# A two-layer transformer block on one core: the norm's root moved to the FFN's eviction, the shift as extra columns, and constant products on TensorE

## The reference

```
def rms_norm(x, w):
    return x * rsqrt(mean(x * x, axis=-1) + 1e-6) * w
def modulate(h, shift, scale):
    return h * (1.0 + scale) + shift
def swiglu(h, w_in, w_out):
    gate, up = split(h @ w_in, 2, axis=-1)
    return (silu(gate) * up) @ w_out
h = h + 0.5 * lm[2] * swiglu(modulate(rms_norm(h, norm_w), lm[0], lm[1]), ffn_w_in, ffn_w_out)
```

## Time and profile before

| | us |
|---|---|
| median of 3 runs | 2743.12 (2735.91, 2743.12, 2744.52) |
| profiled execution, its own time | 2739.12 |
| its span | 2737.2 |
| TensorE matmul busy | 2664.7 (97%) |
| VectorE busy | 1521.2 (56%) |
| ScalarE busy | 692.3 (25%) |
| mean granted TensorE clock | 0.992 of full |

### The profile page before, as it was taken

How to read it: one execution, slowest core, us unless ns; L and a number is a source line. 1 busy time by engine, 2 the same in 40 slices (tenths; PEclk the granted TensorE clock), 3 DMA queues, 4 the chain that set the end, 5 groups by cost and what they waited for, 6 DMA issues and landing times.

```text
span 2737.2 us, 42267 instructions
## 1 busy us (share of the span) xinstructions
PE 2664.7 (97%) x15515; PEld 2290.5 (84%) x15515; DVE 1521.2 (56%) x2621; ACT 692.3 (25%) x1075; POOL 93.7 (3%) x211
## 2 busy tenths in 40 slices
PE   7999999999999999999999999999999989999998
PEld 4888888888877888888888888888887877888886
DVE  5776477534376477626763677247536465543333
ACT  4111111122256221111111311111113345422222
POOL 0000000000034000000000000000000022000000
PEclk8999999999999999999999999999999999999999
DMA  7877477412200177536762577257422200233332
GB/s 228 198 184 185 113 184 184 125 50 79 54 17 2 54 165 185 146 86 159 184 161 58 123 184 175 71 140 184 126 70 84 69 26 17 81 96 100 91 110 81
DMA packets 485795, 316.98 MB, mean 116 GB/s; under 512 B 30588, under 2 KB 483664, under 8 KB 485712
## 3 DMA queue, kind: packets, MB, share of 16 engines
q1 hardware_dynamic: 485712, 315.88, 45.2%
HBM read 313.73 MB, written 2.10 MB: 115 GB/s over the span
## 4 chain that ended last, share of the span: by engine, by line
PE 91%; DVE 4%; ACT 2%; issue 1%; POOL 1%; DMA 0%; SPq 0%; DVEq 0%; ACTq 0%; POOLq 0%
PE pg L709 79%; PE pg L776 4%; PE p L1047 1%; PE pn L1030 1%; PE pg L986 1%; PE p L724 1%; DVE xlo L1640 1%; DVE tnorm L1632 1%; PE pg L867 1%; ACT whi L1155 0%; DVE wlo L1493 0%; PE pg L991 0%; DVE probT L1847 0%; DVE mx L1854 0%; ACT xhi L1244 0%
## 5 line engine op out<-in xcount | busy, mean ns | idle before, releaser
L709 PE MATMUL pg<-xhi,whi 128*128 128x512 f32 (+1 forms) x2856 | 794.5, 347 | 4.1 <-DVE wlo L1493 4.0
L709 PE MATMUL pg<-xhi,wlo 128*128 128x512 f32 (+1 forms) x2856 | 788.6, 344 | 0.0
L709 PE MATMUL pg<-xlo,whi 128*128 128x512 f32 (+1 forms) x2856 | 787.1, 344 | 0.0
L1155 ACT CAST whi<-raw 128x1024 fp32r<-128x1024 f32 (+1 forms) x288 | 321.8, 1118 | 1060.2 <-PE pg L709 1045.9
L1493 DVE TENSOR_TENSOR wlo<-raw,whi 128x1024 fp32r<-128x1024 f32 (+1 forms) x288 | 377.6, 1311 | 350.5 <-ACT whi L1155 347.8
L709 PEld LDWEIGHTS pg<-xhi,whi 128*128 128x128 f32 x2856 | 451.3, 188 | 72.6 <-DVE wlo L1493 5.9
L709 PEld LDWEIGHTS pg<-xlo,whi 128*128 128x128 f32 x2856 | 450.4, 188 | 69.3
L709 PEld LDWEIGHTS pg<-xhi,wlo 128*128 128x128 f32 x2856 | 450.4, 188 | 68.9
L1577 DVE SCALAR_TENSOR_TENSOR part<-ada,cond,part 128x256 f32<-128x256 f32 x960 | 465.3, 485 | 32.7
L1703 DVE SCALAR_TENSOR_TENSOR h<-pg,gcol,h 128x512 f32 (+1 forms) x118 | 71.4, 639 | 442.3 <-PE pg L709 437.5
L709 PE MATMUL pg<-ahi,whi 128*128 128x512 f32 x1100 | 306.1, 346 | 0.0
(11 more groups left out here) (212 smaller groups left out, 1983.4 us busy)
## 6 DMA issues: line engine op xcount, KB each, us to landing
ada<-in_w_ada SPq DMA_DIRECT2D x512, 256.0 KB, 4.2
raw<-in_ffn_w_in SPq DMA_DIRECT2D x176, 512.0 KB, 3.9
raw<-in_ffn_w_out SPq DMA_DIRECT2D x64, 704.0 KB, 4.5
raw<-in_w_in SPq DMA_DIRECT2D x24, 512.0 KB, 3.8
ada_first<-in_w_ada SPq DMA_DIRECT2D x8, 1024.0 KB, 11.9
raw<-in_w_in SPq DMA_DIRECT2D x16, 256.0 KB, 3.5
raw<-in_w_o SPq DMA_DIRECT2D x16, 256.0 KB, 2.8
raw<-in_w_o SPq DMA_DIRECT2D x32, 128.0 KB, 2.9
```

Source lines behind the costliest of these rows:

```text
L709: last = nc.tensor.matmul(pg[s][:, p0:p1], w[:, s, k], v[:, k, p0:p1], start=(k == 0 and n == 0), stop=(k == kt - 1 and n == 2))
L1155: nc.scalar.copy(whi[:, s, 0:nk], raw[:, s, 0:nk]).then_inc(s_whi[s], 1)
```

## The change

For the norms 0, 2 and 3 (`POST`), the operand of the FFN's first product is `h * acol` without the root and the shift; `xhi` and `xlo` get two more columns with the shift vectors (latent and context), so that columns 768 and 769 of `pg` receive `shift @ w_in`. Every matmul of the second token part in these phases has 258 columns in place of 256. The root is multiplied in when the product is read, and the shift product is added as a bias per partition. `square_sums` of part 1 moves behind the whole first token part, and the roots come at the end of the norm on ScalarE. For norm 3, six of the eight tiles of `xhi` and `xlo` are made during the last pair of the phase before (`EARLY_K`); for norm 2, whose `xhi` is still being read by the product before, from the end of its first token part on. The rows of `xhi` and `xlo` grow from 768 to 776 elements.

In the opening ScalarE squares the untransposed input, with a sum per token; VectorE spreads it over a diagonal, so that `square_sums` gives the same; VectorE copies five of six transposed tiles.

`keep_busy` multiplies constants into a PSUM bank that is unused at that time, in a loop of one matmul with 256 columns: 24 turns in the opening, 6 turns ahead of the first pair after each of norms 1 to 5.

```diff
+            def keep_busy(count):
+                with pe.Fori(0, count) as _:
+                    nc.tensor.matmul(pa[1][:, 0:2 * P], ident_r[:, :], window_r.rearrange("p a k -> p (a k)"),
+                                     start=True, stop=True)
             def first_pair(i, t):
...
+                    p1 = product_columns(m, p1) if part_ else p1
...
+                    if part_ == 0:
+                        keep_busy(6)
...
-                        if part_ == 0 and (s, k) == (0, 1):
+                        if part_ == 0 and (s, k) == (order[-1] if m in POST else (0, 1)):
                             square_sums(m, 1)
             def opening_pair(i):
-                first_modulation(0)
                 square_sums(0, 0)
                 square_sums(0, 1)
+                keep_busy(24)
+                first_modulation(0)
                 first_fold(0)
                 first_modulation(1)
...
+            for tt in range(TOK // P):
+                act.wait_ge(s_x[tt // 2], 32)
+                if tt >= 2:
+                    act.wait_ge(s_sq, tt - 1)
+                nc.scalar.activation(sqjunk[tt % 2][:, :], xtok[:, tt, :], ACT.Square, accum_out=ssq[:, tt:tt + 1]
+                                     ).then_inc(s_sq, 1 if tt < TOK // P - 1 else KD - TOK // P + 1)
+            act.wait_ge(s_xT, TOK // P)
+            nc.scalar.copy(h[:, :, TOK - P:TOK], pg[1][:, :].rearrange("p (k t) -> p k t", k=KD)).then_inc(s_free[1], 1)
             split_hi(0, 0, 0)
             split_hi(0, 1, 0)
-            act.wait_ge(s_free[1], 1)
-            for k in range(KD):
-                square(0, k, k % 2, 1)
...
+            def scaled_hi(m, part_, k):
+                nc.scalar.activation(xhi[:, k, p0:p1], h[:, k, p0:p1], ACT.Identity, scale=acol[:, k, v:v + 1]
+                                     ).then_inc(s_xh, 1)
+            def shift_columns_hi(m, k0, k1):
+                nc.scalar.copy(xhi[:, k0:k1, TOK:XB], mod[:, shift + k0:shift + k1, 0:2])
...
+                if m == 0:
+                    for q in range(KD // 2):
+                        if q == 2:
+                            copy_first(2)
+                        act.wait_ge(s_coef, coef_count(0, 2 * q))
+                        shift_columns_hi(0, 2 * q, 2 * q + 2)
+                        for k in (2 * q, 2 * q + 1):
+                            scaled_hi(0, 0, k)
+                            scaled_hi(0, 1, k)
+                        if q == 1:
+                            nc.scalar.preload_act_table_set("natural_log_exp_and_others")
+                            root(0)
+                            root(1)
+                    return
+                if m in POST:
+                    if phases[i][0] == "wo":
+                        act.wait_ge(s_coef, coef_count(m, 0))
+                        for k in range(4):
+                            scaled_hi(m, 0, k)
+                        split_hi(i + 1, 0, 0)
+                        square_part(i, 1, 0)
+                        for k in range(4, KD):
+                            scaled_hi(m, 0, k)
+                        split_hi(i + 1, 1, 0)
+                        square_part(i, 1, 1)
+                        shift_columns_hi(m, 0, KD)
+                        for k in range(KD):
+                            scaled_hi(m, 1, k)
+                    else:
+                        split_hi(i + 1, 0, 0)
+                        square_part(i, 1, 0)
+                        scaled_hi(m, 1, KD - 2)
+                        split_hi(i + 1, 1, 0)
+                        square_part(i, 1, 1)
+                        scaled_hi(m, 1, KD - 1)
+                    nc.scalar.preload_act_table_set("natural_log_exp_and_others")
+                    root(0)
+                    root(1)
+                    return
...
+                        if m in POST:
+                            split_hi(nxt, 0, jn)
+                            act.wait_ge(s_free[0], read_value(i, f))
+                            nc.scalar.activation(gate[:, 0:SEQ], gate[:, 0:SEQ], ACT.Silu, bias=gbias[:, 0:1])
+                            nc.scalar.activation(gate[:, SEQ:TOK], gate[:, SEQ:TOK], ACT.Silu, bias=gbias[:, 1:2]
+                                                 ).then_inc(s_gd, 1)
+                            split_hi(nxt, 1, jn)
+                            return
...
-            for tt in range(1, TOK // P, 2):
+            for tt in range(TOK // P - 1):
                 dve.wait_ge(s_xT, tt + 1)
...
-            for k in range(KD):
-                sum_squares(0, k, k % 2)
+            for b, (t0_, t1_) in enumerate(((0, SEQ // P), (SEQ // P, TOK // P))):
+                dve.wait_ge(s_sq, (SEQ // P, KD)[b])
+                nc.vector.tensor_tensor(rstd[:, t0_ * P:t1_ * P].rearrange("p (a t) -> p a t", t=P),
+                                        ident.unsqueeze(1).broadcast_to([P, t1_ - t0_, P]),
+                                        ssq[:, t0_:t1_].unsqueeze(2).broadcast_to([P, t1_ - t0_, P]), ALU.mult
+                                        ).then_inc(s_acc, KD // 2 + 1)
...
+            def scaled_low(m, part_, k):
+                dve.wait_ge(s_xh, xn_count(m, part_, k))
+                nc.vector.scalar_tensor_tensor(xlo[:, k, p0:p1], h[:, k, p0:p1], acol[:, k, v:v + 1],
+                                               xhi[:, k, p0:p1].bitcast(f32), ALU.mult, ALU.subtract).then_inc(s_xn, 1)
...
+                if m in POST:
+                    if phases[i][0] == "wo":
+                        for k in range(3):
+                            scaled_low(m, 0, k)
+                        add_part(i, 1, 0)
+                        split_lo(i + 1, 0, 0)
+                        scaled_low(m, 0, 3)
+                        sum_part(m, 1, 0)
+                        for k in (4, 5):
+                            scaled_low(m, 0, k)
+                        add_part(i, 1, 1)
+                        split_lo(i + 1, 1, 0)
...
+                        if m in POST:
+                            dve.wait_ge(s_unit[0], f + (j0 + 1))
+                            nc.vector.tensor_tensor(gate[:, :], pg[0][:, 0:TOK], rstd[:, :], ALU.mult)
+                            nc.vector.tensor_copy(gbias[:, 0:2], pg[0][:, TOK:XB]).then_inc(s_free[0], 1)
                         split_lo(nxt, 0, jn)
...
+                        if m in POST:
+                            nc.vector.tensor_copy(gbias[:, 2:4], pg[1][:, TOK:XB])
+                            u = up[:, col, :].rearrange("p o t -> p (o t)")
+                            nc.vector.tensor_tensor(u, pg[1][:, 0:TOK], rstd[:, :], ALU.mult).then_inc(s_free[1], 1)
+                            dve.wait_ge(s_free[1], read_value(i, f))
+                            dve.wait_ge(s_gd, gate_count(m, hf, f))
+                            for v, (p0, p1) in enumerate(((0, SEQ), (SEQ, TOK))):
+                                last = nc.vector.scalar_tensor_tensor(gate[:, p0:p1], u[:, p0:p1],
+                                                                      gbias[:, 2 + v:3 + v], gate[:, p0:p1],
+                                                                      ALU.add, ALU.mult)
...
+                        early = EARLY_K.get(nn, 0)
+                        for part_ in range(2):
+                            if early and part_:
+                                shift_columns_low(nn, 0, KD)
+                            for k in range(early):
+                                scaled_low(nn, part_, k)
```

145 lines of the change are left out of this document (99 added, 46 removed).

## The result

The changed kernel takes 2745.18 us (median of 14 executions, 2743.06 to 2748.41), the kernel before in the same session 2740.93 (14 executions, 2735.66 to 2746.17): ratio 1.0018, 95% interval 1.0011 to 1.0025. The forecast of 2727 and the range up to 2739 missed. By the bound of 0.3% set in the prediction this is no difference; the interval itself says slightly slower, by 3 to 7 us. The profiled executions show the same: spans of 2737.2 before and 2741.9 after.

A forecast was written before the change was run, and what follows sets the result against it. TensorE, busy 97% of the span, was taken as the bound. Terms -7.5 - 5.6 - 3.8 + 2.7 = -14.2 gave 2724.9 from the profiled 2739.1, 2728.9 on the median's scale; forecast set at 2727 us, range 2718 to 2739.

The forecast's parts named there:

- Two more columns, plus 2.7: Part 1 products of three norms: 3168 matmuls, 0.85 ns more each, cost 2.7 us; bounds 0 and 6.3.
- a step over 17.2: Sign of being wrong in the `in` phases: a step longer than 17.2 us, where 17.13 was expected from 17.09.
- Opening, minus 7.5: Opening: earlier square sums, full clock and fewer waits save 7.5 us, first product tile at 33.2; bounds 3.5 and 8.1.
- They end at 24.4 and cost nothing if the loop itself is free: Opening: the 24 constant products take 2.8 us and end before the first `w_ada` piece lands at 24.85.
- Norm 2, minus 5.6: Norm 2: scaling tiles early removes most waits of TensorE and saves 5.6 us; bounds 3 and 6.3.
- Norm 3, minus 3.8: Norm 3: six tiles made during the last pair before it save 3.8 us; bounds 2.5 to 4.4.
- the 1.3 us more: Norms 2 and 3 together: possible extra loss if each constant-product turn paid about 108 ns for compare-and-branch.
- Norms 1, 4, 5: 0: Norms 1, 4 and 5: the six constant products fall into waits, no change; clock could move it 1.7 us either way.
- The eviction: 0: Reading out products: VectorE's added 2.6 us a step fit into its 3.96 us idle time, costing nothing.
- Rival 4: VectorE becomes the bound of the `in` phases, 61 steps grow by 0.5 us: 2762; chance 0.08.
- Rival 2: Opening stays slow: constant products issue slowly and don't lift the clock, gain shrinks by 4: 2731; chance 0.15.
- rival 3: Columns cost 6.3 us, norms 2 and 3 give only 3 and 2.5: 2732 to 2736; chance 0.17.

The follow-up runs named there:

- e4_no24: The changed kernel without the 24 constant products in the opening: 2743.45 us, ratio 1.0015 to the kernel before.
- e7_unroll24: The changed kernel with the opening's 24 constant products written out instead of looped: 2742.63 us, ratio 1.0005 to the kernel before.
- e8_nobusy: The changed kernel without any constant product, neither the opening's 24 nor the six ahead of each first pair: 2743.09 us, ratio 1.0008 to the kernel before.

## Why the prediction was wrong, point by point

**Two more columns, plus 2.7: wrong, and the step that failed most.** The term took a column at 0.43 ns from rows 8 and an upper bound of 6.3 from rows 9. Measured were 12.7 in the six `in` phases. About 6.0 of it are the columns with the rows held (2 ns a matmul, not 0.85; inside the bound). The other 6.7 came with the rows of 3104 bytes, against the faster of the two repeats that rows of 3072 bytes can run in. The step counted what the change adds to a product and never asked what moving the rows from 3072 to 3104 bytes does to every product. Its own sign of being wrong, a step over 17.2, came: 17.30.

**The last FFN: not in the sum.** The prediction listed the norms that change and held the rest at nothing; the wider rows reach every reader of `xhi` and `xlo`. It cost 5.8 us, shown by the run with wider rows alone, by the split rows and by the five runs on that FFN.

**Opening, minus 7.5: measured minus 3.1, below the lower bound of 3.5.** The first product tile starts at 37.31, not 33.2. "They end at 24.4 and cost nothing if the loop itself is free" failed: the first six turns took 0.92 us, probably issued ahead while TensorE waited, the others about 0.4 us each, and the products ended at 30.25. The clock did not stay at 1.00 either: 0.57 from 25 to 30 us. The Trainium skill (Advanced Engine Details and Errata, Control Flow Timing) gives about 108 ns for a compare-and-branch. The trace has more for a whole turn of this loop: 0.40 us, of which the product takes 0.13, so 0.27 for the rest. Without the loop (e4_no24, e7_unroll24, e8_nobusy) the opening gains 4.9 to 5.5, still 2 short: the second piece lands later than the 30.9 allowed (TensorE waits for it until 31.89 in the run with dense products), and ahead of the copy of piece 2 the table load and the two roots stood on the chain for 3.5 us (43.18 to 46.64), priced at 1.1.

**Norm 2, minus 5.6: measured minus 5.4. Norm 3, minus 3.8: measured minus 3.8.** Right, mechanism and size; against the two runs of the kernel before with memory shifted the gains are 6.2, and 4.3 and 4.9. (The term for norm 3 came to 3.7 in the prediction's own sum.) The six constant products took 0.71 us [the chain above, 955.26], 0.12 each, as the row priced them; the 1.3 us more, by which the prediction's sum would have been 12.9, did not come. The difference to the opening is that products were still running when the loop began; that its turns were issued ahead for this reason is a reading, not shown.

**Norms 1, 4, 5: 0, measured +0.1, 0.0, -0.1.** Right, for norm 1 with luck: it takes 45.5 to 47.5 us in the runs, as the clock falls there or not, within the plus or minus 1.7 that the prediction allowed.

**The eviction: 0.** Right. VectorE's added passes stayed under TensorE's products: it is busy for 14.56 of 17.31 us in a step (132.50 to 149.81), where it was 12.36 of 17.09. Rival 4 did not come; VectorE still waits 2.0 us in one piece:

```profile
149.51 0.16 DVE L2057 COPY gbias<-pg 128x2 f32<-128x2 f32 x1 [2.03 <-PE pg L737]
```

**The sum.** Forecast -14.2; with the measured terms -3.1 - 5.4 - 3.8 + 12.7 = +0.4, then +5.8 in the last FFN and -1.4 from the rest: +4.8. Rival 2 (slow loop, low clock) was right in its mechanism, though the first tile took 2.34 and not 3.06; rival 3 in the columns, not in the norms. No rival had the rows, so the range stopped at 2739.

## What to carry to other kernels

Before a tile that TensorE streams is padded, work out where each row begins: here rows that no longer all began a multiple of 256 bytes from the old start cost 2.5% on every product in a stream of 512 columns alone, in a stage whose code the change had not touched. Ask of every changed size who else reads that memory. And fill a wait with products written out rather than in a loop of one, after checking that a load does not bound the same stretch. Last, a stage that comes out at one of two lengths by itself must be seen at both before a change is charged with the difference.

## What the runs showed of the hardware

- Streams of 512 columns alone, rows beginning where they did or multiples of 256 bytes from there (3072, 2304, 2048 apart): 226.7 to 226.8 ns a product. All rows 32 bytes later: 233.3. Distances of 3104, 2176, 2112 or 3136, which put some rows off by 32 to 224 bytes: 231.7 to 232.5.
- Streams of alternating 512 and 256 columns over rows of 3072 bytes run in one of two repeats, 347 or 353 ns a pair of products, with all else equal, and can change between two turns of a loop; 0.32 us in 17. What picks one is open. Over rows of 3104 bytes a pair takes 350 on average.
- A turn of a loop with one product of 256 columns took about 0.4 us in a wait of TensorE (after six faster ones), the same products written out 0.13 each; right behind running products six turns took 0.12 us each.
- Dense constant products kept the granted clock at 1.00 from 25 to 30 us, where it was 0.50 and 0.66 in two runs without them, and 0.57 with the same products in a loop.
- Norm 1 took 45.5 us in the seven runs whose granted clock stayed at 1.00 from 610 to 625 us, and 45.6 to 47.5 in those where it was 0.77 to 0.89, with or without constant products ahead of it.
